# Copies of a transposed activation one product earlier, and three staged loads one job earlier

## What is computed

```
h = rmsnorm(x, g_norm)
u_p, z_p, q, k, v, z_r, gates = split(einsum('bld,de->ble', h, w_in))
y_pool = pooling(u_p) * silu(z_p) @ w_branch_pool
y_ret  = groupnorm(retention(rope(q), rope(k), v)) * silu(z_r) @ w_branch_ret
x_out  = x + (sigmoid(gate_p) * y_pool + sigmoid(gate_r) * y_ret) @ w_out
```

## Time and profile before

| | us |
|---|---|
| median of 3 runs | 3213.09 |
| the three runs | 3206.94 to 3213.5 |
| profiled execution | 3215.49 |
| its span, first to last instruction | 3213.9 |
| PE busy in it | 3018.7 (94%) |
| DVE busy | 1832.5 (57%) |
| ACT busy | 1153.0 (36%) |
| mean granted clock | 0.974 |

### The profile page before, as it was taken

How to read it: one execution, slowest core, us unless ns; L and a number is a source line. 1 busy time by engine, 2 the same in 40 slices (tenths; PEclk the granted TensorE clock), 3 DMA queues, 4 the chain that set the end, 5 groups by cost and what they waited for, 6 DMA issues and landing times.

```text
span 3213.9 us, 36292 instructions
## 1 busy us (share of the span) xinstructions
PE 3018.7 (94%) x13000; PEld 2321.7 (72%) x13000; DVE 1832.5 (57%) x2594; ACT 1153.0 (36%) x1892; POOL 713.5 (22%) x499
## 2 busy tenths in 40 slices
PE   6999999998889999999998999999899999969997
PEld 5888888876778888888876877777787777742222
DVE  7666667563353757566664675565566556634331
ACT  4444443434454444444442333332333323312210
POOL 3343434342232343434340000000000000001110
PEclk8999999999999999999999999999999999979999
DMA  4535353534453444444438455545645653448885
GB/s 131 205 119 196 128 187 133 182 109 147 146 181 120 166 158 164 159 164 154 164 106 321 169 176 213 216 143 209 233 161 180 228 222 110 179 161 312 288 312 192
DMA packets 297599, 582.06 MB, mean 181 GB/s; under 512 B 24840, under 2 KB 167688, under 8 KB 286255
## 3 DMA queue, kind: packets, MB, share of 16 engines
q1 hardware_dynamic: 292039, 562.73, 49.4%
q0 software_dynamic: 5392, 17.12, 1.4%
HBM read 410.63 MB, written 169.50 MB: 181 GB/s over the span
## 4 chain that ended last, share of the span: by engine, by line
PE 75%; DVE 9%; issue 8%; DMA 4%; ACT 2%; POOL 1%; SPq 1%; DVEq 0%; ACTq 0%; POOLq 0%
PE bank L1068 22%; PE bank L1070 21%; PE bank L1069 21%; PE bank L1353 6%; PE bank L1391 2%; PE bank L1116 1%; DMA raw<-in_w_out 1%; DMA raw<-in_w_branch_pool 1%; DVE z_in L2035 1%; DVE win_a L1774 1%; DVE wa_lo L1774 1%; DVE xs L1788 1%; PE bank L1384 1%; DVE win_b L1774 1%; PE bank L1063 1%
## 5 line engine op out<-in xcount | busy, mean ns | idle before, releaser
L1068 PE MATMUL bank<-xa_hi,wa_hi 128*128 128x512 f32 x2240 | 888.7, 397 | 16.4 <-ACT part_v L1498 7.8
L1070 PE MATMUL bank<-xa_hi,wa_lo 128*128 128x512 f32 x2240 | 877.9, 392 | 0.0
L1069 PE MATMUL bank<-xa_lo,wa_hi 128*128 128x512 f32 x2240 | 877.3, 392 | 0.0
L1068 PEld LDWEIGHTS bank<-xa_hi,wa_hi 128*128 128x128 f32 x2240 | 424.6, 190 | 103.6 <-issue 10.3
L1070 PEld LDWEIGHTS bank<-xa_hi,wa_lo 128*128 128x128 f32 x2240 | 423.5, 189 | 89.8
L1069 PEld LDWEIGHTS bank<-xa_lo,wa_hi 128*128 128x128 f32 x2240 | 424.6, 190 | 85.2
L1774 DVE TENSOR_TENSOR wa_lo<-w_raw,wa_hi 128x512 fp32r<-128x512 f32 x320 | 305.6, 959 | 194.8 <-ACT wa_hi L1486 193.9
L1774 DVE TENSOR_TENSOR w_lo<-raw,w_hi 128x512 fp32r<-128x512 f32 (+1 forms) x288 | 181.2, 659 | 257.5 <-ACT w_hi L1592 257.4
L1774 DVE TENSOR_TENSOR wa_lo<-w_sum,wa_hi 128x512 fp32r<-128x512 f32 x240 | 192.0, 800 | 237.5 <-ACT wa_hi L1486 237.2
L1486 ACT ACTIVATE wa_hi<-w_raw 128x512 fp32r<-128x512 f32 x320 | 200.9, 628 | 251.5 <-PE bank L1070 251.5
L1592 ACT ACTIVATE w_hi<-raw 128x512 fp32r<-128x512 f32 (+1 forms) x288 | 166.6, 603 | 303.7 <-PE bank L1070 150.7
(11 more groups left out here) (238 smaller groups left out, 4636.5 us busy)
## 6 DMA issues: line engine op xcount, KB each, us to landing
w_raw<-in_w_in SPq DMA_DIRECT2D x80, 1024.0 KB, 5.2
v_d<-turned SPq DMA_DIRECT2D x64, 512.0 KB, 3.2
qk_s<-qk_d SPq DMA_DIRECT2D x32, 1024.0 KB, 6.9
v_s<-v_d SPq DMA_DIRECT2D x32, 1024.0 KB, 12.0
raw<-in_w_branch_ret SPq DMA_DIRECT2D x128, 256.0 KB, 3.4
s_w<-in_w_in SPq DMA_DIRECT2D x64, 512.0 KB, 4.8
tabs<-in_c_rope SPq DMA_DIRECT2D x16, 1024.0 KB, 5.8
qk_d<-high SPq DMA_DIRECT2D x32, 512.0 KB, 4.6
```

What stands on the lines that cost most here:

```text
L1068: pe.matmul(out, lh, rh, start=first, stop=False, skip_group_check=onto)
L1069: pe.matmul(out, lh, rl, start=False, stop=False, skip_group_check=onto)
L1070: return pe.matmul(out, ll, rh, start=False, stop=last, skip_group_check=onto)
```

## The change

ACT's copies and SP's stores move one product ahead: a copy now stands in the step behind whose product its own transpose is done (offset 4 + k // 2 instead of 5 + k // 2), and the store at 5 + k // 2 instead of 6 + k // 2. PE's transposes stay at 4 + k // 2. The first three loads of the second half's operands move from SP's list of job 39 to the end of that of job 38; the loads 3 to 6 stay where they were. No instruction is added or removed, and none changes its form or its waits.

```diff
@@ -689,11 +689,14 @@
                             norm_row(1)
                         x_rows(n)
                     for k in range(PROD):
-                        n = step(j, i, 6 + k // 2)
+                        n = step(j, i, 5 + k // 2)
                         if n is not None:
                             x_store(n, k)
+                if j == NJ - 2:
+                    for i in range(3):
+                        x_load(i)
                 if j == NJ - 1:
-                    for i in range(PROD):
+                    for i in range(3, PROD):
                         x_load(i)
 
 
@@ -1574,7 +1577,7 @@
                     if n is not None:
                         squares(n)
                     for k in range(PROD):
-                        n = step(j, i, 5 + k // 2)
+                        n = step(j, i, 4 + k // 2)
                         if n is not None:
                             x_copy(n, k)
                     if j == NJ - 1:
```

## The result

| | before | after |
|---|---|---|
| median of the runs, us | 3212.99 | 3186.18 |
| lowest and highest | 3206.94 to 3213.5 | 3184.01 to 3189.1 |
| profiled execution (span) | 3215.49 (3213.9) | 3184.01 (3182.4) |

A forecast was written before the change was run, and what follows sets the result against it. PE, 94% busy, was held by twelve x_out waits (23.1 us), one part_v wait (7.8 us) and low clock behind them. Gains of 21.2 (preparation) and 8.7 (change of halves) made 29.9 us, giving 3183 us; range 3174 to 3195.

The forecast's parts named there:

- change of halves: Jobs 39 to 40, switching to the second half's operands: gain 8.7 us, bounds 6 and 12.4.
- The place of the copies: Pairs 4 to 7: earlier copies remove PE's transpose waits of 7.3, 5.4, 5.7 and 4.7 us, unless something else holds ACT.
- Landing in pair 6: Copy 4 waits for the k = 0 store, landing 7.3 us after issue: new PE wait of 3.1 us.
- Landing in pair 4: Copy 4 wanted at 727.8, store landing about 728.1 with PE at half clock: no wait.
- takes back more: Rival: store landings and low clock in pairs 4, 6 and the change of halves leave gain 20, 3193 us; chance 0.14.
- The rows of pair 6: Rows loaded behind weights and stores: wait of about 2 us on ACT, 1.0 on PE, bounds 0 and 2.2.
- The early loads: Loads 0 to 2 issued in job 38 let ACT cast operand 0 straight behind product 0; the 7.8 us wait goes.
- what is late next: Jobs 39 to 40: loads 3 to 6 wait for low parts; PE's part_s wait of 1.69 becomes about 2.1 us.
- Kept gain: Behind 935 us nothing depends on absolute time, so the whole gain was taken as kept.
- the rival with no new wait in pair 6: Store of k = 0 and rows land in time: gain 35.7, up to 38 us, 3176 us; chance 0.14.
- the preparation: Pairs 4 to 7, copies and stores of x_out before job 39: gain 21.2 us, including 5.0 of clock.

The follow-up runs named there:

- stores first: Changed kernel with the x_out stores of k = 0 to 3 issued ahead of weights and result stores in jobs 33 and 36; 3183.28 us, ratio 0.9898.
- five buffers: Changed kernel with five x_out buffers instead of four, the order of all queues kept; 3184.5 us, ratio 0.9905.
- copies only: Kernel before the change with only copies and stores one product earlier, all seven loads still in job 39; 3197.43 us, ratio 0.9954.
- all first: Changed kernel with stores (job 33), rows of pair 6 (job 35), and stores plus rows of pair 7 (job 36) ahead of each job's transfers; 3172.24 us.
- rows first: Changed kernel with the load of pair 6's rows issued ahead of job 35's weights and stores; 3182.94 us, ratio 0.9897.
- cast late: Changed kernel with ACT's cast of the last new operand moved behind the first eviction and weight cast of job 40; 3188.27 us, ratio 0.9924.
- all first with cast late: Changed kernel with both the reordered transfers of all first and the moved cast of cast late; 3173.17 us, ratio 0.9868.
- loads only: Kernel before the change with only the first three operand loads moved to job 38, copies and stores unmoved; 3206.48 us, ratio 0.9976.

## Why the prediction was right, and where it was not

I said 3183 us from a gain of 29.9, and 3186.2 was measured, with 26.8. In the traces, from first transposes to first transposes of the pairs (for pair 6, which has no wait there, from the eviction in front of them, 795.42 and 782.77), the terms are:

| | predicted | traces |
|---|---|---|
| pair 4 (with its clock, 1.7) | 6.2 | 44.3 to 39.9: 4.4 |
| pair 5 (with clock 1.6, less 1.0 for the rows) | 6.0 | 38.3 to 32.9: 5.4 |
| pair 6 (less 3.1 for the landing, with clock 1.7) | 4.3 | 41.8 to 39.7: 2.1 |
| pair 7 | 4.7 | 41.6 to 36.1: 5.5 |
| change of halves | 8.7 | 9.2 |

**The place of the copies.** Right: nine of the twelve waits went, the one on POOL shrank from 3.3 to 2.78 us (said: 2.8), and the two left have another cause, the landing. Pair 7 gave 5.5 us where the waits added up to 4.7. An explanation that no run tests is that the idle time shown before an instruction leaves out a little at each wait; it would be 0.25 us at each of three.

**Landing in pair 6.** Right in mechanism and place, shown by stores first and by five buffers; the size was off. I took the landing of before, 7.3 us, and the issue at the same distance from PE; it was 8.0 us, from an issue at 789.62 that was 4.0 us ahead of PE's last transposes, not 4.7. The wait was 4.8 us for 3.1. The Trainium skill, page "DMA: Bandwidth & Descriptors", section "Anatomy of one DMA — SWDGE (gpsimd) path", fits a transfer as 2.0 us plus the bytes over 436 GB/s, an estimate of 2.6 us here. The traces agree for the store that goes first (2.8 us); behind 2 MB the fit is three times too short (8.0 us).

**Landing in pair 4.** This step failed. I wrote that the clock would stay at half behind the wait of 2.8 us "as it is now", and that the store would then land just in time: nothing. In the trace of after the clock was 1.00 there, PE came to the last transposes sooner and waited 3.25 us for a store that took 9.4 us, where the time of landing that I used, 728.1, was that of before, with 8.0 us. So three waits for x_out stood where the prediction looked for two. The rival "takes back more" named just this case, at 3 us. In copies only, the clock did fall behind the same wait (0.81 and 0.85 in the two windows from 715), PE waited only 1.33 us, and the pair took 38.0 us, 2.0 less than with the full clock: the slow products lay under the landing, and no slow stretch came after it. The 1.33 us also say that the landing (9.0 us there) would have cost something even with the clock as predicted. That pair 4 still gave 4.4 us of 6.2 is in part luck: its waits fell only from 7.3 to 6.0 us, by 1.3 where I had 4.5, and the rest, 3.1 us, goes mostly with the clock, where I had 1.7.

**The rows of pair 6.** Right: 2.84 us on ACT, 1.98 us on PE (said: 2 and 1.0). ACT's wait was worked out with a landing up to 1 us sooner than before; the two stores that went ahead took nothing from it, it took 9.7 us.

**The early loads.** Right, shown alone: the 7.8 us went, and no cast of the first three waited. For what is late next I said about 2.1 us; it was 2.78, because load 3 landed a microsecond later than I had it. DVE started the low part of operand 0 only at 863.58, behind a weight part that took 1.61 us beside POOL's sums where I had 0.7, so ACT waited 2.16 us and not 1.2. The 1.3 us of slow clock that I took off behind it did not come: 1.00 in every window of that stretch. The first error took 0.7 us and the second gave 1.3, so that 9.2 stands against 8.7.

**Kept gain.** Right as far as the traces tell: from 920 to 1600 us PE is busy for 677.7 of 680 us in both, and in the eight traces of the experiments. From the last event to the end of the span the ten traces take 2293.7 (all first) to 2306.0 us (stores first), in no order of the time saved; before has 2298.1 and after 2295.9. So nothing is seen to be given back, and 12 us of scatter stand behind the stretches that were measured.

**Two sums** of the prediction are slightly off, and neither enters the forecast: the rival with no new wait in pair 6 reaches 35.7 + 1.3 = 37.0 us where the change of halves has no slow clock, not 38; and the bound for the change of halves with no wait at all is 8.7 + 1.3 + 2.1 = 12.1 us, not 12.4.

## What to carry to other kernels

A consumer that frees the buffer of the next but one producer belongs straight behind its own producer: one place too late does not show in the busy share of the engine that is late, and here cost PE 23 us. When a chain gets faster, look up what its transfers stand behind in the issuing queue: 256 KB took 2.8 us in front of a job's 2 MB and 8 to 9 us behind them, and reordering three lists gave 14.3 us in the preparation, where the change had given 17.2 (3.1 us of it went again in the change of halves, until the last cast was moved). Move all the transfers of such a place together, since a single move can hand the wait to the next.

## What was not expected of the hardware

The same wait of 2.78 us in pair 4, at the same place of the same instructions, was followed by a slow window in the traces of copies only (0.81 and 0.85), stores first (0.83 and 0.83), rows first (0.66) and five buffers (0.66), and by none in those of after, all first, cast late, and all first with cast late. The wait near 777 us was followed by slow windows in stores first (1.91 us, 0.66) and five buffers (2.07 us, 0.82), and by none in after (1.98) and copies only (2.05). Before the change I had read the earlier trace rows as "over 2 us falls, under 1.9 does not"; the length of a wait alone does not decide it, and a term for the clock behind a wait of 2 to 3 us should be taken as either nothing or its whole 1.7 us. The waits for part_s in job 40 say the same: 2.78 us was followed by a slow stretch in loads only and 1.94 us in copies only, and 2.78 to 2.95 us by none in after, stores first, rows first and five buffers.

There is a pattern, though. Some 55 us before the first copies of pair 4, where no kernel differs, PE waits 3.2 us for part_s in all ten traces. The wait is followed by a slow stretch in before, loads only, copies only, stores first, rows first and five buffers (0.66 or 0.83 in 660:670), and by none in after, all first, cast late, and all first with cast late (1.00). These are the same six and four traces in which the first long wait of pair 4 (3.30 or 2.78 us) was and was not followed by a slow stretch. The wait and the window in after, and the window in rows first:

```profile
662.12 0.47 PE L1071 MATMUL bank<-xa_hi,wa_hi 128*128 128x512 f32 x1 [3.21 <-ACT part_s L1505]
...
660.00:670.00 10.00, 7.88 (x35) 1.00 0.14 54
...
660.00:670.00 10.00, 6.79 (x18) 0.66 0.14 54
```

So what decides both seems to belong to the execution and not to the edit; each kernel has one trace, so this is not shown apart. The slow stretch behind the first wait is also what makes the clock 0.98 or 0.99 in 500:700. The executions with it come 1.4 to 4.2 us later to the first event, and pair 4 differs between after and copies only, whose code there is the same, by 2.0 us, so that differences of 2 us between two single traces should not be put down to an edit. What decides it stays open.
